# Second mixer: the order of weight casts, ropes and the memory's evacuation around its attention

## The reference, cut to what matters

```python
proj = (hn @ w_qkv + b_qkv).astype(F32)                     # 1024 -> 1536
q = rope(proj[..., :C_Q].reshape(b, s, C_HEADS, C_HD), pos)
k = rope(proj[..., C_Q:C_Q + C_KV]...); v = proj[..., C_Q + C_KV:]...
sc = jnp.where(valid, jnp.einsum('btkgd,bskd->bkgts', qj, kj) * scale, -jnp.inf)
m = jnp.maximum(jnp.max(sc, -1), sink)
pr = jnp.exp(sc - m[..., None]); den = jnp.sum(pr, -1) + jnp.exp(sink - m)
o = jnp.einsum('bkgts,bskd->btkgd', pr / den[..., None], vj)
h = h + post_norm(o @ w_o + b_o)
# second block, for l in (0, 1):
mem_kv = _rms_norm(mem, mem_norm[l]) @ mem_w_kv[l]          # 1024 -> 512
```

## Time and profile before

| | us |
|---|---|
| median of three runs | 1508.3 |
| the profiled execution | 1507.89 |
| its span in the profile | 1506.6 |
| TensorE busy in the span | 1452.7 (96%) |
| VectorE busy | 994.2 (66%) |
| ScalarE busy | 774.3 (51%) |
| GpSimd busy | 108.8 (7%) |

### The profile page before, as it was taken

How to read it: one execution, slowest core, us unless ns; L and a number is a source line. 1 busy time by engine, 2 the same in 40 slices (tenths; PEclk the granted TensorE clock), 3 DMA queues, 4 the chain that set the end, 5 groups by cost and what they waited for, 6 DMA issues and landing times.

```text
span 1506.6 us, 26045 instructions
## 1 busy us (share of the span) xinstructions
PE 1452.7 (96%) x10884; PEld 1378.7 (92%) x10884; DVE 994.2 (66%) x1495; ACT 774.3 (51%) x1219; POOL 108.8 (7%) x100
## 2 busy tenths in 40 slices
PE   7999989999998889999999998999999998999999
PEld 7989989999986789999998788999998788999999
DVE  5575667664687557654486866777756677677763
ACT  6644445444574354443366765544445676644443
POOL 0004111100000001110000000011100000011100
PEclk9999999999999899999999989999999989999999
DMA  8532156556454135655555221655565412265553
GB/s 260 164 112 84 57 165 192 176 177 197 157 197 140 57 112 172 196 172 192 190 162 167 96 84 57 193 168 171 184 195 193 152 57 85 84 186 179 186 185 106
DMA packets 186574, 228.19 MB, mean 151 GB/s; under 512 B 5965, under 2 KB 161229, under 8 KB 186457
## 3 DMA queue, kind: packets, MB, share of 16 engines
q1 hardware_dynamic: 185448, 221.75, 46.0%
q0 software_dynamic: 1008, 4.77, 0.9%
HBM read 225.46 MB, written 1.05 MB: 150 GB/s over the span
## 4 chain that ended last, share of the span: by engine, by line
PE 71%; DVE 18%; ACT 7%; issue 3%; POOL 0%; DMA 0%; ACTq 0%; DVEq 0%; SPq 0%; POOLq 0%
PE bank L495 20%; PE bank L497 19%; PE bank L496 19%; DVE weights_low L786 7%; ACT weights_high L684 3%; PE bank L503 3%; PE bank L1006 2%; PE bank L2052 2%; PE bank L2073 2%; DVE cv L2944 2%; ACT S L2139 2%; DVE cv L2941 1%; DVE S L2200 1%; DVE pad L2931 1%; DVE cv L2950 1%
## 5 line engine op out<-in xcount | busy, mean ns | idle before, releaser
L786 DVE TENSOR_TENSOR weights_low<-weights_raw,weights_high 128x1024 fp32r<-128x1024 f32 (+2 forms) x421 | 507.0, 1226 | 289.0 <-ACT weights_high L684 288.9
L684 ACT CAST weights_high<-weights_raw 128x1024 fp32r<-128x1024 f32 (+2 forms) x421 | 424.6, 1031 | 257.9 <-PE bank L497 256.6
L495 PE MATMUL bank<-hT_high,weights_high 128*128 128x256 f32 x1640 | 471.5, 288 | 10.4 <-DVE hT_low L862 4.8
L496 PE MATMUL bank<-hT_low,weights_high 128*128 128x256 f32 x1640 | 466.6, 285 | 0.0
L497 PE MATMUL bank<-hT_high,weights_low 128*128 128x256 f32 x1640 | 466.4, 284 | 0.0
L495 PEld LDWEIGHTS bank<-hT_high,weights_high 128*128 128x128 f32 x1640 | 316.6, 193 | 16.5 <-issue 9.4
L496 PEld LDWEIGHTS bank<-hT_low,weights_high 128*128 128x128 f32 x1640 | 316.8, 193 | 0.3
L497 PEld LDWEIGHTS bank<-hT_high,weights_low 128*128 128x128 f32 x1640 | 316.5, 193 | 0.2
L495 PE MATMUL bank<-aT_high,weights_high 128*128 128x256 f32 x864 | 241.9, 280 | 0.2
L496 PE MATMUL bank<-aT_low,weights_high 128*128 128x256 f32 x864 | 241.0, 279 | 0.0
L497 PE MATMUL bank<-aT_high,weights_low 128*128 128x256 f32 x864 | 240.8, 279 | 0.0
(11 more groups left out here) (417 smaller groups left out, 1829.8 us busy)
## 6 DMA issues: line engine op xcount, KB each, us to landing
weights_raw<-in_w_up SPq DMA_DIRECT2D x32, 1024.0 KB, 5.4
weights_raw<-in_w_down SPq DMA_DIRECT2D x32, 1024.0 KB, 5.2
weights_raw<-in_ffn_w_gate SPq DMA_DIRECT2D x22, 1024.0 KB, 5.4
weights_raw<-in_ffn_w_up SPq DMA_DIRECT2D x22, 1024.0 KB, 5.3
weights_raw<-in_w_in SPq DMA_DIRECT2D x20, 1024.0 KB, 5.1
weights_raw<-in_w_in_ab SPq DMA_DIRECT2D x16, 1024.0 KB, 5.7
weights_raw<-in_ffn_w_down SPq DMA_DIRECT2D x16, 1024.0 KB, 5.3
weights_raw<-in_w_o SPq DMA_DIRECT2D x10, 1024.0 KB, 5.0
```

The source lines that it names most:

```text
L495: k.E.matmul(out, xh, wh, start=first, stop=False)
L496: k.E.matmul(out, xh, wl, start=False, stop=False)
L684: k.A.copy(w.halves(n)[0], w.raw_part(n)).then_inc(*k.s.weight_high(n))
L786: k.V.tensor_tensor(low, w.raw_part(n), high.bitcast(F32), ALU.subtract).then_inc(*k.s.weight_low(n))
```

## The change

Five things are moved; no operation is added or taken away. Two casts of weights (high and low) go into the memory's turning, ahead of its root. The list of memory splits becomes two, with one more entry each and other steps, one for ScalarE and one for VectorE. The evacuation of the memory's products and the second tile of the late rope go to the front of VectorE's `prepared(n)`, ahead of its casts, by the new argument `first`; the first tile of the late rope goes before the attention.

```diff
 def scalar_memory_turned(k):
...
         last.then_inc(*k.s.turned_high(("mem", c)))
+    scalar_split(k, k.w.first(("qkv_c", 0, 512)) - 2)
     scalar_rms(k, "mem", m.mem, [k.s.memory_landed.at("mem")] * NT, m.inv)
 def vector_memory_turned(k):
...
         last.then_inc(*k.banks.read(("mem", "T", c)))
+        if c >= 4:
+            vector_split(k, k.w.first(("qkv_c", 0, 512)) + c // 2 - 5)
     vector_rms(k, "mem", m.inv)
-MEMORY_SPLITS = (0, 0, 3, 3, 5, 5, 7)
+HIGH_SPLITS = (0, 2, 3, 4, 5, 6, 7, 8)
+LOW_SPLITS = (0, 0, 3, 4, 5, 6, 7, 8)
 def scalar_memory_projected(k):
-    for upto in MEMORY_SPLITS:
+    for upto in HIGH_SPLITS:
 def vector_memory_projected(k):
-    for upto in MEMORY_SPLITS:
+    for upto in LOW_SPLITS:
-def vector_attention(k, a, finish, work=None, between=iter(()), amid=lambda step: None):
+def vector_attention(k, a, finish, work=None, between=iter(()), amid=lambda step: None, first=lambda n: None):
     def prepared(n):
+        first(n)
         next(between, None)
 def vector_mixer_c(k):
-    def turned_heads(c0, n, n0):
-        for t in range(NT):
+    def turned_heads(c0, n, n0, tiles=range(NT)):
+        for t in tiles:
             V.wait_ge(*k.banks.was_read(("c", n0, t)))
...
-        for t in range(NT):
+        for t in tiles:
             x = m.proj[:, t, c0:c0 + n * CHD].rearrange("p (n d) -> p n d", d=CHD)
...
-    def work(n):
-        if n in (2, 4):
-            vector_memory_evacuated(k, n // 2 - 1)
-        if n == 2:
-            turned_heads(512, 8, 512)
+    turned_heads(512, 8, 512, (0,))
+    def first(n):
+        if n == 1:
+            turned_heads(512, 8, 512, (1,))
+        if n in (1, 3):
+            vector_memory_evacuated(k, n // 2)
-    vector_attention(k, k.attention_c, finish, work, vector_memory_projected(k))
+    vector_attention(k, k.attention_c, finish, None, vector_memory_projected(k), first=first)
```

More of the change, by code:

```diff
@@ L2379, in vector_mixer_c @@
         vector_out_gained(k, "c", p, m.u, post_gain(k, 1, 0), b_o)
-    first = k.w.first(("up", 1, 0, 0))
-    vector_add_post(k, "c", m, ("ff1", 1), k.hT, ff1_gain(k, 1), vector_splits(k, first - 1, first))
+    up = k.w.first(("up", 1, 0, 0))
+    vector_add_post(k, "c", m, ("ff1", 1), k.hT, ff1_gain(k, 1), vector_splits(k, up - 1, up))
     vector_pairs_added(k, ("ff1", 1))
```

## The result

The changed kernel takes 1489.56 us (median of 4 runs, 1487.66 to 1490.72), the kernel before 1507.74 us (4 runs): ratio 0.988, 95% interval 0.9868 to 0.9892. It is faster by 18.2 us. The forecast was 1489.5. The profiled execution took 1490.72 us, its span is 1489.4 us.

The account below looks back on a forecast made before the run. TensorE bounds the kernel through three mixer stops and slow clock: 17.1 us (8.4 idle, 8.7 clock and restarts) plus 1.5 from earlier casts is 18.6, less 0.2 for hand-overs; 1507.9 - 18.4 = 1489.5 us, range 1487.5 to 1496.

Parts of the forecast that it names:

- A: Interval: first probabilities turning to group 1's output turning, 35.28 us; as rival: second kvm stop stays, short 0.12, whole 0.07.
- P: Interval from the memory's transposes to the first turning of probabilities; the earlier q8/q9 casts were to save 1.5 us.
- The bound: TensorE, busy 96% of 1506.6 us: three stops (1.4, 4.7, 3.7 us) before the last projections, and slow clock around two.
- Part 1: q8 and q9 casts ahead of the memory's root remove TensorE's 1.4 us stop; gain 1.5 us, bounds 1.3 to 1.6.
- Part 2: Late rope halved: tile 0 before the first scores with 0.3 us slack, tile 1 behind the first maxima; both free.
- Part 3: kvm evacuation before VectorE's low casts: the 4.72 us stop shrinks to 0 to 0.1; second exponentials at 485.6.
- Part 4: Casts one by one around exponentials; VectorE waits 2.8 us for o0 before evacuating the first group's values, the tightest place.
- The sum: 35.28 us from first probabilities turning replaces 52.42, gaining 17.1; with the early casts 18.6, less 0.2 for hand-overs: 18.4.
- B: Rival: TensorE's idle times go but its clock still falls; pays back 8.7 us, 1498; chance 0.06.
- D: Rival: a cast finds its transfer or buffer not ready, ScalarE's exponentials wait, part of the gain goes; no separate chance.
- C: Rival: VectorE becomes the bound in groups 1 to 3; three stops of 8.6 us, 7.4 us over: 1515; chance 0.03.
- The port: GpSimd key copies meeting tile 1's rope: VectorE up to 0.5 us later, TensorE stops 0.4 us, 1489.9; not summed.

Follow-up runs that it names:

- e6: Kernel before, with 38 and 30 unused matmuls filling TensorE's two kvm stops without shortening the waits: 1502.38 us, ratio 0.9965.
- e1: Kernel before, with only the q8 and q9 casts moved ahead of the memory's root: 1507.88 us, ratio 1.0.
- e2: Changed kernel without the two casts moved ahead of the memory's root: 1491.93 us, ratio 0.9889 to the kernel before.
- e5: Changed kernel with both tiles of the late rope together behind the first maxima, ahead of the kvm evacuation: 1494.92 us, ratio 0.9916 to the kernel before.
- e4: Changed kernel with kvm evacuated behind VectorE's low casts again: 1503.02 us, ratio 0.9965 to the kernel before.
- e3: Changed kernel with the old list of splits for both engines, so casts come in batches again: 1490.33 us, ratio 0.9893 to the kernel before.
- e7: Changed kernel with two unused VectorE additions (1.41 us) in each of groups 1, 2 and 3: 1494.45 us, ratio 0.9916 to the kernel before.
- e10: e7 with one entry of VectorE's split list changed, so o0's low cast comes a call later: 1489.87 us, ratio 0.9888 to the kernel before.
- e8: Changed kernel with six unused VectorE additions (4.2 to 4.3 us) in each of groups 1, 2 and 3: 1503.89 us, ratio 0.9977 to the kernel before.
- e9: Changed kernel with 5, 2 and 9 unused matmuls in TensorE's stops at the end of the first and second mixer: 1487.98 us, ratio 0.9875 to the kernel before.

## Why the prediction was right, point by point

The forecast of 1489.5 met the median within 0.1 us. That close a meeting is luck, since single executions of the changed kernel span 3 us; what was predicted rightly is A and P, and why.

**The bound.** TensorE's stops and its clock: right. e6 took the clock apart from the waits: of the gain in A, 16.91 us, 8.4 are the waits of the earlier trace rows and the rest clock and restarts, of which e6 found 8.1 by itself.

**Part 1.** Forecast 1.5 us (1.3 to 1.6), measured 1.35 in P. The tenth that I added for the restart wasn't there. What the prediction did not consider is that this gain need not show in the time while the later stops are there (e1: 0.9 us lost over P and A together in the one profile, and a median that did not move; e2: 2.4 us between the medians).

**Part 2.** Tile 0 ended ahead of the first scores, with VectorE idle 0.46 us (forecast slack 0.3). e5 shows what the halving is worth, 5 us.

**Part 3.** Forecast stop 0 to 0.1 us at the two `kvm` evacuations, measured none in the list. The second exponentials were forecast at 485.6, and came at 486.34, in an execution that was 0.6 us later when it came to the mixer. e4 shows that this order carries half of the change in A and three quarters in the medians (9.0 and 13.5 us).

**Part 4.** The wait of 2.8 us for o0 came as forecast, and the place behind it is the tightest: in e3 the evacuation came 1.33 us later after the first turning (494.99 - 479.08 against 493.35 - 478.77), and the last four score matmuls of the turn started 0.9 us later (495.79 - 491.94 against 494.56 - 491.62, counted from the second turning of probabilities). So the slack was 0.4 us. The prediction's times left 0.65 (wanted at 493.8, there at 493.15), and the expectation of e7 counted 0.3. e10 shows that it is the wait, not VectorE's work, that makes it so.

**The sum.** A was forecast as 35.28 and is 35.51, P and A together as 18.6 and are 18.26; the 0.2 that I took off for hand-overs was the right size.

**Rivals.** A and B didn't happen. B, that the clock falls though the idle times go, has 1.00 from 452 to 538 against it. The Trainium skill's page (TensorE: Matmul & The Clock Gate, "A second HAM failure mode: psum-queue depth-cycling") speaks of brief stops that come often; no run here shows that. What e6 and e7 show is that a single listed stop of 1.2 or 1.9 us for a PSUM bank was followed by a slow stretch. D didn't happen either: in the changed kernel ScalarE's high casts wait only for TensorE's products, for no transfer (the line below, 436 to 562 us: total, times, longest), and ScalarE stood idle 1.72 us ahead of the first exponentials. C was tested in e8: I had priced it at 8.6 us a stop, three stops, 25.8 us for 3 us in each turn. At 4.2 us in each turn it cost 14.3, 9.5 of them idle (priced at 11.1) and 4.6 clock and restarts in A (priced at 14.7). The step that was over-priced is the clock: a stop does not always bring a whole slow stretch with it.

```profile
ACT weights_high L684 <- PE bank L497: 12.9, 8, 1.9
```

**The port.** GpSimd's pairs of copies, in order of time, against 0.75 and 0.53 us in the earlier trace rows:

```profile
464.37 2.24 POOL L2400 COPY k<-proj 128x128 f32<-128x128 f32 x2 [18.12 <-PE bank L503]
476.19 1.19 POOL L2400 COPY k<-proj 128x128 f32<-128x128 f32 x2 [9.58 <-PE bank L503]
```

Both now lie beside VectorE's operations on two SBUF operands and take longer, as the rule (SBUF — State Buffer, "Who interferes with whom", of the Trainium skill) says. But it was almost wholly GpSimd that waited. From the start of its first to the start of its last operation VectorE's rope took 1.82 us beside the copies (475.78 to 477.60), against 1.74 for tile 0 without them (469.03 to 470.77): 0.1 us, and not the 0.4 that I worked out by the rule.

## What to carry to other kernels

Where one engine both releases buffers and prepares operands, put the release first, and never behind a wait for a third engine: moving the evacuation ahead of three casts, with no operation saved, is 9.0 us of 18.3 in the profiles and 13.5 of 18.2 in the medians here (e4), and one moved cast repaid a loss of 4.6 us (e7 to e10). Count a stop of TensorE by what runs slow behind it as well, but only where TensorE sets the pace. Gains of stops need not add up one by one: taking away the first of three did not move the median while the other two stood, and in the profile the slow work behind those two grew by more than it had saved.

## What the runs showed of the hardware that was not expected

The clock's answer to a stop is not a matter of the stop's length alone. A stop of 1.36 us in the kernel before left it at 1.00; one of 1.20 us in e6 (0.62 over 502 to 506, the first line) and one of 1.79 us in e5 were followed by a slow stretch, and 0.54 us in e3 was not. Two stops of the same listed length, 1.88 us, went different ways: in e7 the clock fell within it and stayed at 0.50 until 502.6 (the second line), in e8 it stayed at 1.00 through the stop (the third line) and until 500.4. The same stop of 3.7 us had the clock down at its end in e1 and only 1 to 2 us after it in the kernel before. And in e9 it fell in the second mixer with the stops filled.

```profile
502.00:506.00 4.00, 3.91 (x10) 2.82 (x11) 3.96 (x9) 0.15 (x1) 0.00 (x0) 0.62 0.54 219
...
496.00:498.00 2.00, 1.87 (x4) 1.17 (x4) 2.00 (x5) 0.00 (x0) 0.00 (x0) 0.50 0.01 4
...
486.00:488.00 2.00, 0.14 (x2) 0.00 (x0) 1.97 (x4) 0.00 (x0) 0.00 (x0) 1.00 0.09 37
```

So the cost of one stop, read from one profile, is good to about a microsecond or two (e1 and the kernel before differ by 0.99 and 1.28 us at the same two stops), while the work at full clock repeats to 0.04 us.
